# Expert weights loaded in the order in which they are used, and the products of a batch reordered

## What is computed

```python
p_group = softmax(h @ w_router_group);  g_idx, g_gate = argmax, max of p_group
logits  = (h @ w_router_expert) of group g_idx          # 8 experts a group
top_vals, top_idx = top_k(logits, 2)                     # two experts for each token
comb    = one_hot(g_idx) * softmax(top_vals) * g_gate    # a weight for each token and expert
for e in all 32 experts:                                 # hidden width 512
    act = silu(h @ w_gate[e]) * (h @ w_up[e]) * comb[:, e]
    y  += act @ w_down[e]
```

## Time and profile before

| | us |
|---|---|
| median of three runs | 1581.9 |
| the profiled execution's own time | 1581.37 |
| its span, first to last instruction | 1579.6 |
| TensorE busy | 1449.9 (92%) |
| VectorE busy | 856.2 (54%) |
| ScalarE busy | 605.2 (38%) |
| bytes read from HBM | 393.83 MB |

### The profile page before, as it was taken

The page is one execution under the profiler, slowest core; times in us unless marked ns, Lnnn a source line. Parts: engine busy times, 40 slices in busy tenths (PEclk is TensorE's granted clock), DMA queues, the critical chain, the costliest instruction groups (busy, mean ns, idle before and its releaser), DMA issues.

```text
span 1579.6 us, 26831 instructions
## 1 busy us (share of the span) xinstructions
PE 1449.9 (92%) x10856; PEld 1135.6 (72%) x10856; DVE 856.2 (54%) x1140; ACT 605.2 (38%) x787; POOL 33.1 (2%) x69
## 2 busy tenths in 40 slices
PE   8999999999999999999999999999976777766767
PEld 7888888888888888877788888778644434434434
DVE  5777688577776777755457776777611101101101
ACT  5444465563445544466554444664200000000001
POOL 4000000000000000000010000010000000000000
PEclk9999999999999999999999999999988878789879
DMA  7565544456564565554356555477999999999994
GB/s 242 195 211 187 191 156 134 133 177 216 166 211 160 187 209 189 173 180 138 122 165 213 186 178 193 162 237 282 406 427 427 428 429 428 430 429 427 429 429 160
DMA packets 150197, 396.67 MB, mean 251 GB/s; under 512 B 8132, under 2 KB 106516, under 8 KB 136833
## 3 DMA queue, kind: packets, MB, share of 16 engines
q1 hardware_dynamic: 148576, 392.20, 66.8%
q0 software_dynamic: 1440, 3.72, 1.0%
q10 hardware_dynamic: 128, 0.03, 0.0%
HBM read 393.83 MB, written 1.05 MB: 250 GB/s over the span
## 4 chain that ended last, share of the span: by engine, by line
PE 73%; DMA 21%; DVE 3%; ACT 2%; issue 1%; SPq 0%; DVEq 0%; POOL 0%; ACTq 0%; POOLq 0%
DMA early_pair<-in_w_exp_down 21%; PE psum L558 17%; PE psum L259 12%; PE psum L261 12%; PE psum L260 12%; PE psum L564 9%; PE psum L2403 3%; PE psum L2376 1%; PE psum L1025 1%; DVE low L254 1%; PE psum L2348 1%; PE psum L1436 1%; PE psum L2412 1%; DVE hT L446 1%; ACT hT L436 0%
## 5 line engine op out<-in xcount | busy, mean ns | idle before, releaser
L254 DVE TENSOR_TENSOR low<-raw,high 128x2048 fp32r<-128x2048 f32 x179 | 409.6, 2291 | 193.4 <-ACT high L250 192.9
L250 ACT ACTIVATE high<-raw 128x2048 fp32r<-128x2048 f32 x179 | 341.4, 1910 | 125.0 <-PE psum L564 90.1
L558 PE MATMUL psum<-hT,high 128*128 128x512 f32 x1152 | 288.0, 392 | 0.1
L558 PEld LDWEIGHTS psum<-hT,high 128*128 128x128 f32 x1152 | 209.3, 189 | 39.4 <-DVE low L254 0.5
L259 PE MATMUL psum<-high,hT 128*128 128x512 f32 x496 | 200.0, 403 | 6.9 <-DVE low L254 4.5
L261 PE MATMUL psum<-high,hT 128*128 128x512 f32 x496 | 194.5, 392 | 0.0
L260 PE MATMUL psum<-low,hT 128*128 128x512 f32 x496 | 193.9, 391 | 0.0
L564 PEld LDWEIGHTS psum<-hT,low 128*128 128x128 f32 x1152 | 157.2, 190 | 11.2
L564 PE MATMUL psum<-hT,low 128*128 128x256 f32 x1152 | 160.6, 282 | 0.0
L259 PE MATMUL psum<-high,aT_high 128*128 128x512 f32 x352 | 137.9, 392 | 0.2
L260 PE MATMUL psum<-low,aT_high 128*128 128x512 f32 x352 | 137.4, 390 | 0.0
(11 more groups left out here) (358 smaller groups left out, 1574.2 us busy)
## 6 DMA issues: line engine op xcount, KB each, us to landing
pair_ring<-in_w_exp_gate SPq DMA_DIRECT2D x24, 2048.0 KB, 25.1
pair_ring<-in_w_exp_up SPq DMA_DIRECT2D x24, 2048.0 KB, 29.6
raw<-in_ffn_w_gate SPq DMA_DIRECT2D x88, 512.0 KB, 4.0
raw<-in_ffn_w_up SPq DMA_DIRECT2D x88, 512.0 KB, 4.9
raw<-in_ffn_w_down SPq DMA_DIRECT2D x88, 512.0 KB, 4.4
early_pair<-in_w_exp_down SPq DMA_DIRECT2D x16, 2048.0 KB, 25.5
extra_pairs<-in_w_exp_up SPq DMA_DIRECT2D x8, 2048.0 KB, 22.6
pair_ring<-in_w_exp_down SPq DMA_DIRECT2D x8, 2048.0 KB, 17.4
```

The costliest lines, as they stand in the source:

```text
L250: act.activation(high[:, p % RING, :], raw_of(p), ACT.Copy).then_inc(rounded, 1)
L254: dve.tensor_tensor(low[:, p % RING, :], raw_of(p), high[:, p % RING, :].bitcast(F32), ALU.subtract).then_inc(split, 1)
L558: pe.matmul(to.rearrange("p (o n) -> p o n", o=2), w_high, both_parts, start=kk == 0, stop=False, skip_group_check=True)
```

## The change

Three things are moved; no instruction is added or taken away, apart from one wait.

SP in the loop (batches 1 to 6) issued G0, G1 (next), D2 (own), G2 (next), D3 (own), G3, D0, D1 (next). Now it issues D2, D3 (own), G0, G1, D0, G2, G3, D1 (next), so that the transfers come in the order in which TensorE uses them. Batch 0 keeps the old order of loads.

TensorE does gu3 and the gather ahead of d1. A batch was gu0 gu1 d0 gu2 d1 gu3 gather d2 d3 and is gu0 gu1 d0 gu2 gu3 gather d1 d2 d3. The wait for the copies of the gather goes from d2 to d1, and `turn_inner(j + 1)` now stands ahead of `scatter(j)` for j = 1 and 2. ScalarE and VectorE follow in their order of work.

The numbers of the events follow from that: the product that frees the place of G3 is now the fifth of the batch and no longer the sixth, and d1, which frees the place of D3, is the sixth and no longer the fifth.

```diff
-        BOTH_AT, DOWN_AT = [1, 2, 4, 6], [3, 5, 7, 8]
+        BOTH_AT, DOWN_AT = [1, 2, 4, 5], [3, 6, 7, 8]
...
-            def reload(b):
+            both(0, 0)
+            both(1, 0)
+            own_down(2, 0)
+            both(2, 0)
+            own_down(3, 0)
+            both(3, 0)
+            next_down(0, 0)
+            next_down(1, 0)
+            n = last_batch(sp)
+            with sp.Fori(1, n) as c:
+                b = (c, 0)
+                own_down(2, b)
+                own_down(3, b)
                 both(0, b)
                 both(1, b)
-                own_down(2, b)
+                next_down(0, b)
                 both(2, b)
-                own_down(3, b)
                 both(3, b)
-                next_down(0, b)
                 next_down(1, b)
-
-            reload(0)
-            n = last_batch(sp)
-            with sp.Fori(1, n) as c:
-                reload((c, 0))
             own_down(2, (n, 0))
             own_down(3, (n, 0))
...
             def down(j, b):
                 pe.wait_ge(e["a_sb"], at(b, TILES, j + 1))
-                if j == TILES - 2:
+                if j == 1:
                     pe.wait_ge(e["x_sb"], at(b, 2, 4))
...
                 gate_up(2, b)
                 scatter(0, b)
                 turn_inner(1, b)
-                down(1, b)
                 spread_shares(1, b)
+                pe.wait_ge(e["a_sb"], at(b, TILES, 2))
                 gate_up(3, b)
-                scatter(1, b)
-                turn_inner(2, b)
                 pe.wait_ge(e["shares_sb"], at(b, 2, 2))
                 for half in range(2):
                     turn_half(half, following)
+                down(1, b)
+                turn_inner(2, b)
+                scatter(1, b)
                 down(2, b)
+                turn_inner(3, b)
                 scatter(2, b)
-                turn_inner(3, b)
                 down(3, b)
...
             def batch(b, following):
                 silu(0, b)
-                for j in (1, 2):
-                    silu(j, b)
-                    result(j - 1, b)
+                silu(1, b)
+                result(0, b)
+                silu(2, b)
                 silu(3, b)
                 for half in range(2):
                     rows(half, following)
-                for j in (2, 3):
+                for j in (1, 2, 3):
                     result(j, b)
...
                 picks_of(dve, next_picks)
+                inner(3, b)
                 inner_turned(2, b)
-                inner(3, b)
                 inner_turned(3, b)
```

## The result

The changed kernel takes 1603.22 us (median of four runs, 1601.22 to 1607.86), the kernel before 1582.92 us (four runs: the three behind the 1581.9 us of the start, and one of 1584.62). The ratio is 1.0137, with a 95% interval of 1.0124 to 1.0150: 20 us slower. The profiled execution took 1602.88 us, its span 1601.1 us, 21.5 us longer than the span before.

A forecast was written before the change was run, and what follows sets the result against it. The weight stream (DMA) was taken as the bound, with TensorE some 15 us slack a batch; 13.5 + 20 - 12.6 = +20.9 us gave span 1600.5 and time about 1602.5 us, range 1593 to 1616.

The forecast's parts named there:

- The crossing in batch 1: Change from old to new load order: D3 of batch 1 lands late, since only D1 and D2 are queued; 13.5 us, once.
- the unbroken stream of the forecast: Batch 1's reference without a stall: transfers land 4.9 us apart, so D3 would land at 1202.7 us.
- The steady stall: Batches 2 to 6: D3 waits for d1 behind gu3 and the gather, the queue runs dry; 4.0 us each, 20 us together.
- The bare step: In each of batches 2 to 6, D3 lands 13.2 us behind D1 instead of 9.8; 3.4 us lost.
- the allowance of 0.6 us for a late gu3: Added per batch in batches 2 to 6 in case gu2 or gu3 runs at half clock; bounds 0 to 3.6 us.
- The tail: From the landing of the last batch's D1 to the end of the span: 21.4 us instead of 34.0, 12.6 us gained.
- T: The time at which D1 of a batch lands; for batch 7, 1545.6 us before and 1579.1 us forecast.
- The price of a load into an empty queue: D3 issued with nothing ahead takes 7.9 us to land, 3.0 us more than a transfer with another just ahead.
- the queue never runs dry: Rival, faster: D3 lands 9.8 us behind D1 and only the gain at the end is left; 1569 us, chance 5%.
- only at the crossing: Rival, same: the loss in batches 2 to 6 is hidden and only batch 1's 13.5 us remains; 1582.5 us, chance 4%.
- The low clock: Rival, slower still: gu3 runs at half clock in each batch, 3.6 us more in batches 2 to 7; about 1621 us, 13%.
- the forecast's own range: 1597 to 1611 us: 0 to 1.8 us of late gu3 a batch and 0.5 us on each landing.

The follow-up runs named there:

- the order that is 0.6 to 0.8% faster than the kernel before: Against the kernel before: products gu0 gu1 d0 d1 gu2 d2 gu3 d3, loads in order of use; 1572.4 us; with clock held outside batch 0, 1570.14 us.

## Why the prediction was right

The forecast was 1602.5 us, the median is 1603.2, and the steps can be compared one by one. All landings below are those of D1, issue plus time to landing: 1177.29 + 17.5 = 1194.8 (batch 1), and likewise 1267.8 (2), 1331.5 (3), 1579.3 (7). In the kernel before these landings were 59.2 us apart from batch 1 to batch 2 and 58.7 us in all later batches.

**The crossing in batch 1.** Worked out: 13.5 us. Measured: from D1 to D1 of the next batch 73.0 us instead of 59.2, 13.8 us. D2 was issued at 1192.08 and D3 at 1210.14, 18.1 us apart, as said. D3's second half came 8.7 us after the first issue and not 7.9; that the kernel before itself lost 0.5 us in this batch, which the unbroken stream of the forecast left out, nearly makes up for it. In batch 0 nothing was lost, as forecast: G0 of batch 1 was issued 1.9 us later than before (1131.43 instead of 1129.50), and D1 of batch 1 landed 1.9 us later.

**The steady stall.** Worked out: 4.0 us in each of batches 2 to 6. Measured: 63.7 us for batch 2 and (1579.3 - 1331.5) / 4 = 61.95 for the others, so 5.0 and four times 3.25. The sum is 18.0 us instead of 20. The bare step, 3.4 us, was right within 0.2. The part of it that was mis-sized is the allowance of 0.6 us for a late gu3: in batches 3 to 6 gu3 began with its load's landing and took 3.66 us, at the full clock, and in batch 2 it took 5.35 us, at a granted clock of 0.68. The timeline of this one slow case:

```profile
1262.99 5.35 PE L2381 MATMUL psum<-pair_ring,gain 128*32 128x256 f32 x64 [1.28 <-DMA pair_ring<-in_w_exp_up]
1268.26 3.84 PE L2353 MATMUL psum<-route_tables,h 128*128 128x128 f32 x32
1272.79 1.93 PE L2408 MATMUL psum<-pair_ring,levels 128*32 128x256 f32 x32 [0.69 <-ACT gain L2481]
```

**The tail.** Worked out: T + 21.4 instead of T + 34.0, 12.6 us gained. Measured: 1601.1 - 1579.3 = 21.8, and 12.2 us gained.

**The sum.** 13.8 + 18.0 - 12.2 = 19.6 us, and with the 1.9 us by which G0 was issued later in this execution the 21.5 us by which the spans differ. The forecast had 20.9 us and nothing for G0. The 1.9 us do not belong to the change: in the changed kernel with the doubled gather G0 was issued at 1129.80. The terms were off by +0.3, -2.0 and +0.4 us and the sum by -1.3, so the 0.7 us between forecast and median is in part luck.

**The price of a load into an empty queue** was 7.9 us by the rows. In batch 3 it was 7.4 (1337.01 to 1344.4). The estimate of 6.8 us by the figures of the Trainium skill (DMA: Bandwidth & Descriptors, Anatomy of one DMA) is lower than each of the values here, 7.4 to 8.7. That section gives its figures for DMAs issued by GpSimd, while all loads here are issued by SyncE.

**The rivals.** The queue did run dry, in every batch, so "the queue never runs dry" and "only at the crossing" are out. The low clock reached gu3 in one batch of the seven, although gu2 ahead of it took 5.0 to 6.4 us instead of 3.66 in each of batches 2 to 7, and what batch 2 lost more than the others, 1.8 us, is the upper end of what the forecast's own range allowed for a late gu3. The gathers stayed at 3.8 us.

The kernels with the doubled gather and with the old loads show that the mechanism is the right one, and not only its sum: the first raises the loss by the work added, the second takes the whole of it away.

## What to carry to other kernels

Where a stream of loads is the bound, what matters for each load is what lies between it and the product that frees its place: count the transfers issued ahead of it that do not depend on that product, and compare them with the work on the path to it. Loads in the order of use are good only if every place comes free that long before its turn; here, with D1, D2 and D3 loaded one behind the other into two places, each of the three orders of the products that were tried lost 1.7 to 3.2 us in a usual batch. Behind the last transfer the opposite holds, and there the work left to do is the price: both together led to the order that is 0.6 to 0.8% faster than the kernel before.

## What the runs showed of the hardware

D3 that was issued 2.3 us behind the landing of D1, with 2.6 us of D2 still to come, landed 9.8 to 10.3 us after its first issue in nine of ten batches (2 to 6 of two kernels), in one transfer or in two halves, and 8.1 us after it in the tenth. Into an empty queue the same load took 7.4 to 7.9 us in batches 2 to 7 of the changed kernel and 8.6 to 8.9 us in batch 1 of five kernels. So most of what an issue 3.2 us sooner should give was lost: D3 landed 12.0 to 12.5 us behind D1, where it landed 12.9 to 13.2 us behind it in batches 3 to 6 of the changed kernel. What decides it was not found, for D2 of batch 1, issued 2.1 to 2.7 us ahead of D1's landing in five kernels, took 8.4 to 8.6 us in each.

A pause of 4.86 us on TensorE before the last gate and up product of the new order cost 2.5 us in that product (6.2 us at a granted clock of 0.59, instead of 3.66), and 14 matmuls of the identity in the pause took it away (granted clock from 1160 to 1540 us 0.94 instead of 0.91).
